# A fused two-block kernel on one core: four small re-orderings around the gated-delta stage and the forget-gate rows

## The reference, cut to what matters

```
proj = h @ w_in                                   # A: 4096 + 2048 + 32 columns
q, k, v = split(silu(causal_conv(qkv)))           # z, b, a are the other columns
q, k = l2norm(q) * 128**-0.5, l2norm(k)           # 8 heads of 128, used by 16 value heads
g = cumsum(-exp(A_log) * softplus(a + dt_bias))   # in chunks, here of 128 tokens
T = inverse of (I + strict lower part of (beta k) k^T * decay)
...                                               # u = T v, w = T k, state, output
o = rmsnorm(o) * silu(z);  o @ w_out

proj = h @ w_in                                   # B: 4 x 1024 + 16 columns
cum = cumsum(log_sigmoid(f + f_bias))             # 16 "forget rows", one for each head
logits = q k^T + cum_t - cum_s, causal softmax, times v, times silu(z)
```

## Time and profile before

| what | us |
|---|---|
| median of 3 runs (lowest, highest) | 1737.56 (1735.99, 1741.98) |
| the profiled execution's own time | 1735.53 |
| its span, first to last instruction | 1733.8 |
| PE / DVE / ACT / POOL busy | 1653.8 / 1177.9 / 922.7 / 435.5 |
| chain that ended last, by engine | PE 74%, DVE 12%, "issue" 5%, DMA 4%, ACT 3% |

### The profile page before, as it was taken

How to read it: one execution, slowest core, us unless ns; L and a number is a source line. 1 busy time by engine, 2 the same in 40 slices (tenths; PEclk the granted TensorE clock), 3 DMA queues, 4 the chain that set the end, 5 groups by cost and what they waited for, 6 DMA issues and landing times.

```text
span 1733.8 us, 34333 instructions
## 1 busy us (share of the span) xinstructions
PE 1653.8 (95%) x11657; PEld 1528.1 (88%) x11657; DVE 1177.9 (68%) x2369; ACT 922.7 (53%) x1713; POOL 435.5 (25%) x344
## 2 busy tenths in 40 slices
PE   7999989999999988999999999999999999999998
PEld 5999778888988868988999999989999988888886
DVE  4785378887445557458646999979888755555554
ACT  2765523333445555456445444479898755555554
POOL 3000042442000000500004777776565400000000
PEclk9999989999999999999999999999999999999999
DMA  9655301012834324533754555555444466666663
GB/s 300 217 179 184 121 25 50 24 48 81 260 98 146 122 86 126 172 98 122 187 114 117 166 169 169 169 159 146 132 137 135 153 196 192 192 192 192 194 192 132
DMA packets 211809, 255.54 MB, mean 147 GB/s; under 512 B 15912, under 2 KB 193804, under 8 KB 211724
## 3 DMA queue, kind: packets, MB, share of 16 engines
q1 hardware_dynamic: 211723, 254.39, 48.5%
HBM read 253.29 MB, written 1.05 MB: 147 GB/s over the span
## 4 chain that ended last, share of the span: by engine, by line
PE 74%; DVE 12%; issue 5%; DMA 4%; ACT 3%; SPq 2%; DVEq 1%; ACTq 0%
PE ps L2042 21%; PE ps L2576 20%; PE ps L2558 9%; DMA raw<-in_u_experts 3%; PE ps L2546 3%; PE ps L2062 2%; DVE raw L1813 2%; PE ps L2198 2%; PE ps L2289 2%; PE ps L2209 2%; PE ps L2210 2%; SPq L547 1%; PE ps L2130 1%; PE ps L2356 1%; DVE w_lo L1253 1%
## 5 line engine op out<-in xcount | busy, mean ns | idle before, releaser
L675 POOL TENSOR_TENSOR w_lo<-raw,w_hi 128x1024 fp32r<-128x1024 f32 x128 | 307.4, 2405 | 335.3 <-ACT w_hi L1131 335.3
L2042 PE MATMUL ps<-x_hi,w_hi 128*128 128x256 f32 x1088 | 312.9, 288 | 7.6 <-DVE x_lo L1361 3.1
L2042 PE MATMUL ps<-x_lo,w_hi 128*128 128x256 f32 x1088 | 308.4, 283 | 0.0
L2042 PE MATMUL ps<-x_hi,w_lo 128*128 128x256 f32 x1088 | 308.3, 283 | 0.0
L2001 DVE TENSOR_TENSOR w_lo<-raw,w_hi 128x1024 fp32r<-128x1024 f32 x124 | 152.0, 1226 | 143.3 <-ACT w_hi L1231 143.3
L1231 ACT ACTIVATE w_hi<-raw 128x1024 fp32r<-128x1024 f32 x124 | 131.6, 1061 | 167.9 <-PE ps L2576 167.9
L2042 PEld LDWEIGHTS ps<-x_hi,w_hi 128*128 128x128 f32 x1088 | 209.3, 192 | 11.8 <-issue 5.1
L2042 PEld LDWEIGHTS ps<-x_lo,w_hi 128*128 128x128 f32 x1088 | 209.5, 193 | 0.3 <-issue 0.2
L2042 PEld LDWEIGHTS ps<-x_hi,w_lo 128*128 128x128 f32 x1088 | 209.2, 192 | 0.0
L1131 ACT ACTIVATE w_hi<-raw 128x1024 fp32r<-128x1024 f32 x128 | 134.9, 1054 | 119.9 <-DVE raw L1813 119.8
L2521 PE MATMUL ps<-x_hi,w_hi 128*128 128x256 f32 x576 | 166.7, 289 | 10.3 <-ACT arena L1153 10.0
(11 more groups left out here) (394 smaller groups left out, 3850.7 us busy)
## 6 DMA issues: line engine op xcount, KB each, us to landing
raw<-in_u_experts SPq DMA_DIRECT2D x512, 128.0 KB, 2.7
raw<-in_v_experts SPq DMA_DIRECT2D x128, 512.0 KB, 4.3
arena<-in_ada_w SPq DMA_DIRECT2D x22, 1024.0 KB, 5.5
raw<-in_a_w_in SPq DMA_DIRECT2D x12, 1024.0 KB, 5.3
arena<-in_a_w_in SPq DMA_DIRECT2D x12, 1024.0 KB, 5.3
raw<-in_b_w_in SPq DMA_DIRECT2D x8, 1024.0 KB, 5.5
arena<-in_b_w_in SPq DMA_DIRECT2D x8, 1024.0 KB, 5.6
raw<-in_w_in SPq DMA_DIRECT2D x8, 1024.0 KB, 5.5
```

Of the source, the lines that this page charges most:

```text
L675: pool.tensor_tensor(UTL[e], UT[e % 2], UTH[e].bitcast(F32), ALU.subtract).then_inc(utl_ready, 1)
L2042: ins = mm(o[:, b * S:b * S + S], w[:, slot, kk, b * P:b * P + P], xx[:, (kk + turn) % KC, :], start=(kk == 0 and n == 0), stop=(kk == k - ...
```

## The change

It has four parts. (1) ACT's squares of heads 0 and 1 are issued in the z loop, ahead of the wait for the last product and of the last Silu; because the ones that follow on PE no longer lie behind ACT's own wait for `tail_dve`, PE gets that wait in its four iterations. (2) POOL waits once, ahead of its eight passes, for the first two masks of round 0 (`h_pm`). (3) DVE runs `keys(Round(0))` ahead of `gates`. (4) In mixer B `hi(5)` on ACT and `lo(5)` on DVE are issued ahead of the forget rows.

```diff
@@ gpsimd @@
             pool.tensor_tensor(WLO[:, 0, :, :], RAW[0], WHI[:, 0, :, :].bitcast(F32), ALU.subtract).then_inc(lo_ready, 1)
+            pool.wait_ge(h_pm, 2)
             with pool.Fori(0, GQ) as i:
@@ scalar @@
+            def squares_a(j, g):
...
             for u in range(8):
                 if u < 7:
                     hi(T_AIN + 16, 0, u + 2)
+                else:
+                    act.wait_ge(cv_out, 16)
+                    act.sem_inc(g_ln, 2)
+                    for g in range(2):
+                        squares_a(g, g)
                 product(T_AIN + 16, 0, u)
                 act.activation(ZB[:, 2 * u:2 * u + 2, :], bank(T_AIN, u)[:, :], ACT.Silu).then_inc(bank_free, 1)
...
-            act.wait_ge(cv_out, 16)
-            def squares_a(j, g):
...
-            act.sem_inc(g_ln, 2)
-            for g in range(2):
-                squares_a(g, g)
             with act.Fori(0, GQ // 2 - 1) as i:
                 norms_a(i)
@@ scalar, mixer B @@
+            hi(T_BIN, 0, 5)
             exp_and_ln()
             act.wait_ge(b_y, 1)
...
-            for n in range(4, 6):
-                hi(T_BIN, 0, n + 1)
-                evict_b(n)
+            evict_b(4)
+            hi(T_BIN, 0, 6)
+            evict_b(5)
@@ vector @@
             begin(Round(0))
+            keys(Round(0))
             v.wait_ge(bias_in, 32)
             v.wait_ge(raw_free, 8 + N_ADA)
             gates(0, (ps[3], ps[5]))
-            keys(Round(0))
             decays(Round(0))
@@ vector, mixer B @@
             lo(T_BIN, 0, 4)
+            lo(T_BIN, 0, 5)
             v.wait_ge(b_g, 3)
...
-            for n in range(5, 8):
+            for n in range(6, 8):
                 lo(T_BIN, 0, n)
@@ tensor @@
                     mm(ps[6 + g][:, :], ones, SQ[g], start=True, stop=True).then_inc(g_sum, 1)
+                pe.wait_ge(tail_dve, 7)
                 pe.wait_ge(raw_in[2 + i % 2], 16 * (T_AOUT // 4 + i // 2))
                 gate_rows(RAW[2 + i % 2], ps[3 + 2 * (i // 2)], i)
```

More of the change, by code:

```diff
@@ L806, in _ @@
             silu(0, 15)
+            def squares_a(j, g):
+                act.activation(SQ[g][:, 0:256], BLK[:, bass.ds(j, 1), :], ACT.Square).then_inc(g_sq, 1)
+                act.activation(SQ[g][:, 256:512], BLK[:, bass.ds(j + 8, 1), :], ACT.Square).then_inc(g_sq, 1)
             for u in range(8):
@@ L815, in _ @@
             act.activation(EGT, NGT[:, 1, :], ACT.Exp, scale=-1.0).then_inc(tail_act, 1)
-            act.wait_ge(cv_out, 16)
-            def squares_a(j, g):
-                act.activation(SQ[g][:, 0:256], BLK[:, bass.ds(j, 1), :], ACT.Square).then_inc(g_sq, 1)
-                act.activation(SQ[g][:, 256:512], BLK[:, bass.ds(j + 8, 1), :], ACT.Square).then_inc(g_sq, 1)
             def norms_a(i, more=True):
```

## The result

| what | before | after |
|---|---|---|
| median | 1737.87 us (6 runs) | 1728.01 us (6 runs; 1727.36 for the five undisturbed) |
| ratio, after to before | | 0.9941, 95% interval 0.9924 to 0.9958 |
| profiled execution, own time | 1735.53 | 1732.28 |
| its span | 1733.8 | 1730.5 |

The median fell by 9.9 us (1727.6 was forecast), 0.6%, which is more than the 0.3% that can be told from no change. One of the changed kernel's six runs was disturbed (3271.40 us); the ratio and all that follows leave it out. Measured a second time, side by side on one chip, the changed kernel gave 1727.75 against 1738.83, ratio 0.9935 (0.9921 to 0.9949). But the profiled execution is only 3.3 us shorter than the one before, and is the slowest of its kernel's undisturbed runs (the fastest was 1724.53).

A forecast was written before the change was run, and what follows sets the result against it. PE, busy 95% of the span, bounds the kernel; gains come only where it stands or runs slowly. 3.8 + 0.6 + 2.5 + 2.2 = 9.1 us off 1735.53 gives 1726.4, plus 1.2 is 1727.6; range 1723.5 to 1733.0.

The forecast's parts named there:

- The gate tiles' loads: Third and fourth gate tile loads take 5.0 us and are wanted some 6.9 us later, so they stay hidden.
- ACT's first Ln: After the last Silu: possible at about 188.9, needed only near 192.2 by the next sums, so not late.
- C: Round 0, `setup_rows` to `setup_x0`: `lowers` and `starts` free of POOL contention, gain 2.0 us.
- D: Round 0, `setup_x0` to the first `level_d`: gain 0.8 us at the lower clock, 2.1 at full clock.
- F: First `level_d` to the next round's `setup_rows`: `begin(1)` meets POOL and costs 1.5 us, bounds 0 and 3.0.
- the lock rule: In `begin(1)`, each of four DVE instructions could wait out a whole POOL instruction: 2.9 us in all, gain 1.4 less.
- E: Round 0, first to second `level_d`: gain about 1.2 us with the clock returning during the level, up to 1.8.
- a second low spell behind `begin`: Round 0's third level: late `begin` widens PE's gap, clock falls, two levels cost 3.6 us; 1731.2, chance 0.15.
- The clock kept: Rival: clock stays up through the 2.8 us gap before `setup_x0`, 1.9 us more gain, 1725.7; chance 0.25.
- The table loads: Rival: squares between two Silus bring two loads of 1.28 us, moving all behind by 0.6 us; 1728.2, chance 0.07.
- The lower clock: Rival, round 0 from `setup_x0`: lower clock not given back, ten levels cost 18 us, net 9 slower, 1745.7; chance 0.03.
- the POOL rival: POOL's passes cost more in round 0: gain 5.5 us, 1731.2, chance 0.15; the range's end puts it on a higher base.

The follow-up runs named there:

- part 2 alone: Kernel before plus only POOL's single wait for the first two masks: median 1736.42 us, ratio 0.9991 (0.9981 to 1.0).
- tiny sums: Changed kernel with all 120 POOL sums cut to one column, leaving out mixer B's shift and scale (no candidate): median 1725.27 us, ratio 0.9924.
- The parts alone: Kernel before with one part each: medians 1734.51 (part 1), 1736.42 (part 2), 1736.77 us (part 4); part 3 in one execution, 1735.19.

## Why the prediction was right, point by point

- **Part 1: 3.8 forecast, 3.7 measured.** 2.2 us of waiting and the rest from the clock, which stayed up over the 0.34 us that PE now waits: 1.5 us for the 1.8 forecast. The new wait for `tail_dve`, for which 0.1 was taken off, cost nothing: an iteration takes 5.17 us with it and without. The gate tiles' loads and ACT's first Ln stayed hidden.
- **Part 3: 0.6 forecast, 0.62 measured.**
- **Part 4: 2.2 forecast, 2.5 measured.** `lo(6)` stayed in time, and the forget rows ended on DVE at 527.6, 11 us ahead of the first logits. But the prediction saw nothing that would swallow a gain further on, and there the heads' last stretch gave back about 1.8 us in most traces.
- **Part 2: 2.5 forecast, 1.2 and 1.4 measured** (C + D + F in the two traces, against the kernel before; against the changed kernel without POOL's wait it is -0.3 to 1.8 by the trace that one takes). The steps that don't hang on the clock came out: 2.0 in C, and `begin` 1.4 us longer for 1.5 forecast, so the traced contention was the right price and the 2.9 us that the lock rule in the Trainium skill ("SBUF — State Buffer", section "SBUF: two separate sides") would allow was too much. D gained 1.9 in one trace and 1.3 in the other, for 0.8, and E 0.3 and 1.1, for 1.2: the clock fell, as I had taken it, but behind `setup_x0` rather than ahead of it. What failed is the weight of a rival: I gave 0.15 to a second low spell behind `begin`, and both traces of the changed kernel and the one of part 2 alone have it. It costs 1.4 us (F 16.68, against 13.91 with tiny sums, less the 1.37 of `begin`). I priced it at two levels, 3.6 us; it covered one. (The pair at line 1470 that the prediction calls additions are multiplications; the price read from them stands.)
- **The sum.** 9.1 forecast. The steps measured in the changed stages make 3.7 + 0.6 + 1.2 + 2.5 = 8.0 us; the median moved 9.9. With the 1.8 us that the heads give back, 6.2 are left, and the whole span of the second trace is 6.4 us shorter than the one before (1727.4 against 1733.8). So the mechanism of each part held, but that the total came out within 1 us of the forecast is in part luck: part 2 was worth less and the heads took some back, and low spells elsewhere, which the prediction had no term for, made up for it. One of them is at 427.9 to 434.7 before, 6.8 us long:

```profile
427.90:434.70 6.80, 6.29 (x27) 6.00 (x28) 3.84 (x7) 0.99 (x4) 0.00 (x0) 0.50 1.09 360
```

  The stretch from the last `setup_rows` to the end of the rounds takes 45.5 us there and 42.9 and 44.3 in the traces of the changed kernel. Against that, the heads' stretch went from 96.3 to 97.2 and 98.1. And the spell at 761 of the profiled execution made its stage 198.9 us long where the one before has 195.0 and the second trace 195.2: these 3.6 to 3.9 us are why that execution shows 3.3 us of gain and not 7.
- **Trace and median.** The medians fell by 9.9 and 11.1 us, the second trace's span by 6.4. The mean granted clocks explain more than half of what lies between. Worked out from them, the 45 executions of the kernel before that lie beside the experiments spent 39 us on the mean at the lower level, the profiled one 31; the ten of the changed kernel spent 30. Among those 45 each us at the lower level goes with 0.34 us of time. So the profiled execution of the kernel before is a quick one, by some 2.6 us, for its clock alone.
- **Open.** In which stages the other executions of the kernel before lose this time, and whether the changed kernel is spared it by luck or by the shift. The parts alone gave 3.5, 1.6 and 1.2 us in the medians and 0.6 in the trace (part 3), 6.9 together, against 9.9 to 11.1 for the change; with intervals of 0.1% on each, some 2 us, they don't contradict each other and don't settle it.
- **The other rivals.** The clock kept (0.25) did not happen by itself, and when forced was worth, in D and E together, 1.4 us against the first trace and 1.3 against the second, besides the second low spell. The table loads did not happen. The lower clock did not stay: in every trace it came back inside round 0. One sum in the prediction is off: the POOL rival on the higher base is 1737.56 - 5.5 = 1732.1, not the 1733.0 at which the range ends; nothing hangs on it.

## What to carry to other kernels

An engine that shares SBUF with another should get its spare work where the other reads PSUM or has cover; the work needs about 10 us here, so its start must be chosen by where it ends, and one semaphore earlier (scores instead of masks) was worth 1.9 to 2.7 us of the stretch by the traces. Ask of each wait of PE that remains not only how long it is, but whether the clock falls behind it: in part 1 a removed wait of 2.2 us was worth 3.7, in part 4 one of 2.2 us was worth 2.5 on the spot and mostly under 1 by the end, since a low spell came up 100 us later. Where a change is worth 2 to 4 us of 1730 and runs spread over 4 to 8, measure distances between fixed instructions in the traces, and leave the median to the sum.

## What the runs showed of the hardware that I had not expected

- The clock behind a gap of PE of about 2 us is not settled by its length: at the fourth `level_p` it fell behind 1.89, 1.88 and 2.06 us and stayed up behind 2.14, 1.85 and 1.87. One wait of 2.18 us in a stage that no part touches was followed by the lower level in the changed kernel's first trace (line 2360, the spell at 761) and not in the kernel before (line 2356, window after it at 1.00):

```profile
761.32 0.80 PE L2360 MATMUL ps<-arena 128*128 128x128 f32 x2 [2.18 <-DVE arena L1637]
```

```profile
767.47 0.49 PE L2356 MATMUL ps<-arena 128*128 128x128 f32 x2 [2.18 <-DVE arena L1634]
```

  Behind the 2.8 us ahead of `setup_x0` it fell in all five traces that had the gap.
- Two executions of one program differed by 1.9 us within 50 us of the trace (G 48.42 and 50.29), 1.5 of it by the clock.
- A DVE instruction with one operand in PSUM was not slowed by POOL at all (line 1501 before takes 0.69 us each from 252.8 to 257.8, with POOL running, and 0.69 at 232.0, with POOL idle), one with two in SBUF took 0.75 for 0.33 from start to start.
